# Reading five pair tiles before the last experts, and summing two token tiles at a time on four quarters of TensorE

## The reference

```
h = rmsnorm(x, g_ffn)
# router: top group of 4, then the top 2 of its 8 experts; gates w2 from two softmaxes
act = silu(h @ w_gate[e]) * (h @ w_up[e]) * gate     # 32 experts, 1024 -> 128
x = x + sum over the token's two experts of act @ w_down[e]      # 128 -> 1024
y = x * rsqrt(mean(x * x) + 1e-6) * g_final
```

## Time and profile before

| | |
|---|---|
| median of 3 runs | 610.31 us (609.31 to 610.90) |
| the profiled execution | 608.55 us |
| its span, first to last instruction | 606.5 us |
| busy share of the span | PE 94%, PEld 78%, DVE 73%, ACT 40%, POOL 15% |
| chain that ended last | PE 51%, DVE 17%, DMA 7%, issue 3%, ACT 2% |
| HBM | 96.36 MB read, 21.86 MB written |

### The profile page before, as it was taken

How to read it: one execution, slowest core, us unless ns; L and a number is a source line. 1 busy time by engine, 2 the same in 40 slices (tenths; PEclk the granted TensorE clock), 3 DMA queues, 4 the chain that set the end, 5 groups by cost and what they waited for, 6 DMA issues and landing times.

```text
span 606.5 us, 9765 instructions
## 1 busy us (share of the span) xinstructions
PE 571.4 (94%) x3401; PEld 473.4 (78%) x3401; DVE 439.9 (73%) x749; ACT 242.2 (40%) x389; POOL 88.5 (15%) x136
## 2 busy tenths in 40 slices
PE   8899999999999999899999995899997999999775
PEld 6799999997899889688888874777654768887222
DVE  4937997999999696746666658899731667786285
ACT  6642112222212427322222116576322567775443
POOL 4300000200000000100000000433331334431000
PEclk9999999999999999999999997899998999999889
DMA  8761210131112202455422107699989999962697
GB/s 317 150 123 38 69 36 1 36 93 35 36 36 79 105 36 69 114 203 198 157 80 93 54 36 247 215 332 404 392 329 412 407 352 395 394 241 97 209 421 299
DMA packets 52598, 111.27 MB, mean 183 GB/s; under 512 B 10867, under 2 KB 29176, under 8 KB 51449
## 3 DMA queue, kind: packets, MB, share of 16 engines
q1 hardware_dynamic: 44773, 92.18, 43.2%
q0 software_dynamic: 7168, 17.84, 8.2%
q10 hardware_dynamic: 596, 0.50, 0.3%
HBM read 96.36 MB, written 21.86 MB: 195 GB/s over the span
## 4 chain that ended last, share of the span: by engine, by line
PE 51%; DVE 17%; DMA 7%; issue 3%; ACT 2%; SPq 1%; POOL 0%; POOLq 0%; DVEq 0%; ACTq 0%
PE ps L2259 14%; PE ps L2081 9%; PE ps L2425 6%; PE ps L2364 3%; PE ps L2386 3%; PE ps L2400 3%; PE ps L2401 3%; PE ps L2402 3%; DMA at_opair_p<-scratch_out 3%; DMA at_wlater<-in_expert_w_down 3%; DVE at_mixP L1360 3%; PE ps L2496 2%; PE ps L2323 2%; DVE at_hT L1319 1%; DVE at_lnsq L1546 1%
## 5 line engine op out<-in xcount | busy, mean ns | idle before, releaser
L2081 PE MATMUL ps<-at_hT,at_ring 128*128 128x384 f32 x936 | 165.5, 333 | 0.0
L2081 PEld LDWEIGHTS ps<-at_hT,at_ring 128*128 128x128 f32 x936 | 155.9, 188 | 5.1 <-issue 5.0
L2259 PE MATMUL ps<-at_hT,at_mring 128*128 128x512 f32 (+1 forms) x432 | 102.7, 393 | 2.0 <-DVE at_mring L1514 1.3
L2259 PEld LDWEIGHTS ps<-at_hT,at_mring 128*128 128x128 f32 (+1 forms) x432 | 77.3, 182 | 21.3 <-DVE at_mring L1514 1.7
L1360 DVE SCALAR_TENSOR_TENSOR at_mixP<-at_uc,at_par,at_mixP 128x1024 f32<-128x1024 f32 x60 | 77.1, 1285 | 2.1
L2400 PE MATMUL ps<-at_whi,at_hTm 128*128 128x256 f32 x176 | 51.0, 290 | 0.0
L2402 PE MATMUL ps<-at_whi,at_hTm_lo 128*128 128x256 f32 x176 | 49.1, 279 | 0.0
L2364 PEld LDWEIGHTS ps<-sb_ident,at_xg 128*128 128x128 f32 x232 | 29.3, 192 | 18.2 <-issue 15.2
L1795 DVE TENSOR_TENSOR at_wlater_lo<-at_wlater,at_whi 128x1024 fp32r<-128x1024 f32 x30 | 36.7, 1225 | 6.0 <-ACT at_whi L988 5.1
L2425 PE MATMUL ps<-at_wlater,at_actT 128*128 128x512 f32 (+1 forms) x92 | 38.0, 597 | 0.7 <-ACT at_actT L1003 0.7
L988 ACT ACTIVATE at_whi<-at_wlater 128x1024 fp32r<-128x1024 f32 x30 | 31.6, 1055 | 7.3 <-PE ps L2402 6.5
(11 more groups left out here) (324 smaller groups left out, 919.2 us busy)
## 6 DMA issues: line engine op xcount, KB each, us to landing
at_wlater<-in_expert_w_gate SPq DMA_DIRECT2D x20, 512.0 KB, 11.1
at_wlater<-in_expert_w_up SPq DMA_DIRECT2D x20, 512.0 KB, 12.8
at_wlater<-in_expert_w_down SPq DMA_DIRECT2D x20, 512.0 KB, 15.4
at_raw<-in_w_in SPq DMA_DIRECT2D x16, 512.0 KB, 4.0
at_opair_p<-scratch_out SPq DMA_DIRECT2D x8, 1024.0 KB, 14.7
at_wfirst<-in_expert_w_gate SPq DMA_DIRECT2D x12, 512.0 KB, 9.0
at_wfirst<-in_expert_w_up SPq DMA_DIRECT2D x12, 512.0 KB, 10.0
at_wfirst<-in_expert_w_down SPq DMA_DIRECT2D x12, 512.0 KB, 12.5
```

What stands on the lines that cost most here:

```text
L2081: mm = pe.matmul(ps[:, bank + r, 0:t1 - t0], w[:, wpart, k * P:(k + 1) * P], hT[:, hpart, k, t0:t1], start=(m, wpart, hpart) == (0, 0, 0), ...
L2259: mm = pe.matmul(ps[0:n, b + r, :], mring[:, 1 - i % 2, mpart, k * P:k * P + n], wo[:, wpart, k, r * 512:(r + 1) * 512], start=(c, mpart, ...
```

## The change

1. **Early reads.** SP no longer reads all pairs after `moe_done`. `HELD` = 4: once the scatters of blocks 0 to 24 have landed, it reads the pairs of tiles 0 to 4 (`EARLY`), tile 4 also after block 25's down product. POOL waits for these five reads before it scatters block 25. The outputs of blocks 26 and 27 go to buffers of their own (`kept`) instead of `outb`, and the last four scatters always take 128 rows.
2. **Late rows.** Once everything has landed, POOL gathers into the same tiles those tokens' pairs that had an output in the last four blocks (`late_pairs`, five indirect DMAs of 8 KB rows, by the list `later`; other tokens have an index out of bounds and are skipped). VectorE makes the list in blocks 14 to 16 (`pair_turns`, `pair_latest`, `pair_lists`). SP reads tiles 8, 7, 5, 6 (`WHOLE`) after `moe_done` as before.
3. **A filled scratch.** Since rows are read before they are all written, SP first fills `orow` with rows of the inputs: ten DMAs from HBM to HBM behind the pieces 5 to 13, eight of 1 MB and two of 256 KB.
4. **Quarters.** All eight prompt tiles are summed on TensorE, two at a time: (0, 1), (2, 3), (4, 7), (5, 6). As the diagonal matrix and the identity are zero off the diagonal, only the 64 x 64 blocks on it are used: quarter (q, n) multiplies rows 64q to 64q + 63 of tile n of the couple into PSUM partitions 64n to 64n + 63 of double bank 2c + q. A bank so holds half of one tile and half of the other, and each result tile is written by two DMAs of 64 rows. Only tile 8 stays on VectorE.
5. **Gates** are computed in block 17, and ScalarE makes 16 diagonals right behind the last block's output; a one-element copy on VectorE (`dve_clear`) lets TensorE begin with `own_rows`.

The core of the diff:

```diff
-FINAL = [8, 0, 1, 2, 3, 4, 7, 5, 6]
-PE_TILES = [0, 2, 4, 5, 6]
-DVE_TILES = [8, 1, 3, 7]
+COUPLES = [(0, 1), (2, 3), (4, 7), (5, 6)]
+SUMMED = [i for couple in COUPLES for i in couple]
+EARLY = [0, 1, 2, 3, 4]
+WHOLE = [8, 7, 5, 6]
+HELD = 4
...
+            for p in range(2, NPIECE):
+                load_piece(p)
+                if 5 <= p < 14:
+                    fill_out(p - 5)
...
+            b = NB - HELD - 1
+            for k in range(2):
+                sp.wait_ge(scat[k], 16 * ((b + 2 - k) // 2))
+            for i in EARLY:
+                if i == SUMMED[4]:
+                    sp.wait_ge(s["d_done"], b + 2)
+                load_pairs(i)
...
             sp.wait_ge(s["moe_done"], 1)
-            for i in FINAL:
+            for i in WHOLE:
+                load_pairs(i)
...
+                if b == NB - HELD + 1:
+                    for i in EARLY:
+                        pool.wait_ge(pair_in[i], 16)
                 if b >= 1:
                     scatter(b - 1, columns(b - 1)[1])
...
+            def late_pairs():
+                pool.wait_ge(s["turns_ready"], 1)
+                for i in EARLY:
+                    g.indirect_dma_start(opair(i), None, pairs,
+                                         bass.IndirectOffsetOnAxis(ap=later[:, i:i + 1], axis=0),
+                                         bounds_check=last_token, oob_is_err=False).then_inc(pair_late[i], 16)
...
             with pool.If(total < 1):
                 all_scattered(NB)
+                late_pairs()
...
+            def quarters(couple, h, stationary, moving, **flags):
+                for q in range(2):
+                    p = slice(q * 64, q * 64 + 64)
+                    for n in range(2):
+                        mm = pe.matmul(sum_banks(2 * couple + q)[n * 64:n * 64 + 64, h, :],
+                                       stationary(n)[p, p], moving(n)[p, :], **flags)
+                return mm
...
+            own_rows(0)
             own_rows(1)
+            for c, couple in enumerate(COUPLES):
+                if c >= 2:
+                    pe.wait_ge(s["y_done"], 2 * c - 1)
+                    own_rows(c)
+                for i in couple:
+                    pe.wait_ge(pair_in[i], 16)
+                    if i in EARLY:
+                        pe.wait_ge(pair_late[i], 16)
+                pe.wait_ge(s["dg_ready"], 4 * c + 4)
                 for h in range(2):
                     for k in range(2):
                         q = k * D + h * 512
+                        mm = quarters(c, h, lambda n: dg[:, 2 * c + n, k, :],
+                                      lambda n: opair(couple[n])[:, q:q + 512], start=False, stop=k == 1)
```

More of the change, by code:

```diff
@@ L294, in build_layer @@
         order = at("order", [P, 8, REST], o_state + 2304)
+        both = at("both", [P, TILES, 2, NE], o_state)
+        turn = at("turn", [P, NE], o_state + 2304)
+        latest = at("latest", [P, TILES, 2], o_state + 2304 + 192)
+        done_by = at("done_by", [P, TILES], o_state + 2304 + 288)
+        token = at("token", [P, TILES], o_state + 2304 + 384)
+        later = at("later", [P, TILES], o_state + 2304 + 672, I32)
+        no_over = at("no_over", [P, 1], o_state + 2304 + 736)
         eid = at("eid", [1, REST], o_state + 3072, I32)
@@ L374, in build_layer @@
         pair_in = [sem(f"pair_in{i}") for i in range(TILES)]
+        pair_late = {i: sem(f"pair_late{i}") for i in EARLY}
         def wait_piece(eng, p):
@@ L1285, in _ @@
                 all_scattered(NB)
+                late_pairs()
             over_from(0)
+            with pool.If(total > 0):
+                pool.wait_ge(s["moe_done"], 1)
+                late_pairs()
         @block.vector
```

238 lines of the change are left out of this document (135 added, 103 removed).

## The result

The changed kernel is slower: 623.0 us median of 4 runs (619.11 to 626.11) against 610.19 (609.31 to 610.9); the ratio is 1.0207, 95% interval 1.0146 to 1.0269. The profiled execution took 619.11 us with a span of 617.4; before it was 608.55 and 606.5.

What follows compares the result with a forecast made beforehand. It took the 43 us serial tail as bound by reads, then TensorE; `moe_done` +5.5 and a tail behind it of 37.7 against 39.1 gave span 610.6 (+4.1), so 614.4 us from the median 610.31; range 608 to 620.5.

Steps and rivals of the forecast that it cites:

- Early reads in at 564.9, held scatters: Last blocks: early reads take 15.5 us, then four held scatters go back to back; `moe_done` at 572.9, 5.5 us later.
- A gather beside the reads lands in 7.4 us: After `moe_done`: tile 1's gather, issued about 574.4 beside SP's reads, lands 7.4 us later, so couple 0 starts at 581.8.
- Quarters, four at once: TensorE's tail sums: four quarters run at once, 3.44 us for a couple's 32 rows, 1.72 for its own rows.
- Half clock in couple 0, 2.1 us: TensorE at couple 0: a slow clock after 11 us of idling adds 2.1 us, making the sum 5.5.
- The chain couple, norms, own rows: Tail: couple 2's own rows wait for couple 0's two norms (4.6 us); couple 3 ends at 602.3, last norms at 606.9.
- The last write, 3.55: End of span: two DMAs of 64 rows, 3.1 us plus 0.45 for the second issue, ending at 610.5.
- What costs nothing: Ahead of the tail: filling `orow` costs 0; the gather list on VectorE 0 to 0.5 us, taken as 0.1.
- 0.1 that I had allowed on VectorE: Blocks 14 to 17: making the list for the gathers was taken to cost 0.1 us, from a range of 0 to 0.5.
- within 0.3%: Rival for the tail, chance 0.23: reads land in 14.1 us and the gather in 3.8, giving 609.5 us.
- faster: Rival, chance 0.17: early reads in by 562.6, `moe_done` at 567.4 to 569, low gather, no cold clock; 606.4 us.
- Row halves do not take turns: Denies a rival for TensorE's quarters, chance 0.08: row halves take turns, adding 16.1 us, 630 us.
- the change does what it says: Denies a rival, chance 0.02: blocks overflow, so the gathers would be of every token.

Runs made afterwards that it cites:

- early_two: The changed kernel with two tiles (0, 1) read early instead of five, the other seven read whole after `moe_done`: 616.25 us, ratio 1.0114.
- no_early: The changed kernel without early reads, held scatters and gathers; quarters, diagonals and filled rows stay: 612.95 us, ratio 1.0044.
- warm: gathers_first plus eleven unused whole float32 matmuls on TensorE between the own rows of couples 0 and 1: 616.61 us, ratio 1.0094.
- gathers_first: The changed kernel, but SP, after reading tile 8, waits for the five gathers to land before reading tiles 7, 5, 6: 615.93 us, ratio 1.0099.
- halves: The kernel before, but each prompt tile is written by two DMAs of 64 rows instead of one of 128: 611.39 us, ratio 1.0029.
- control: The changed kernel once more, nothing edited: 622.88 us, ratio 1.0218.
- last_couple: The kernel before with quarters only for tiles 5 and 6, in banks of their own, written in 64-row pieces: 612.28 us, ratio 1.0059.
- patched_last: The changed kernel with two early tiles (0, 1) summed late, tile 1 last, whole-tile sums as before and 128-row writes: 610.26 us, ratio 1.0014.

## Why the prediction was off

1. **Early reads in at 564.9, held scatters.** Right. POOL went on at 565.59. The four scatters came 1.3 us apart, and the last took 4.52 instead of 3.94. `moe_done` came at 574.01 instead of 572.9: +1.1 us. early_two and no_early show that this hold is the only reason for it being late.
2. **A gather beside the reads lands in 7.4 us.** This is the step that failed, by size. Tile 1's was issued at 575.62 instead of 574.4 and took 11.77; couple 0 started at 587.63 instead of 581.8. Of these 5.8 us the landing is 4.4 and the issue 1.2. I had taken the gathers of activations beside weight reads the earlier trace rows. The cause is the reads (6.30 us with only tile 8's beside it). What sets them apart from weight reads stays open between two things that the runs didn't part: their pieces of 8 KB for a partition and the megabytes queued at once. With both made smaller my figure is nearly met (8.34). The Trainium skill (DMA: Bandwidth & Descriptors, SWDGE vs HWDGE vs iDMA) says that an engine takes turns between the two kinds of queue, and I had read that as half of the engines for POOL. The trace shows no even shares, 4.2% of the time against 71.1% in the first 6 us, and not by count either, 37 packets against 167.
3. **Quarters, four at once.** Right: 3.43 a couple at full clock, 1.72 to 1.95 for its own rows.
4. **Half clock in couple 0, 2.1 us.** Right in kind: 0.50 and 0.55 in 585 to 591. Couples 0 and 1 took 8.60 us, against 7.10 in warm, so it cost 1.5 here and 2.33 in gathers_first. The sum at 586.28 in the earlier trace rows lost 5.40 - 3.70 = 1.7, not the 2.1 that I took.
5. **The chain couple, norms, own rows.** Right: from couple 0's start to the last norm's end I had 606.9 - 581.8 = 25.1 us, and measured 612.72 - 587.63 = 25.1. That it agrees to a tenth is luck: couple 0 itself was 0.3 shorter than I had it, the norms and the last two couples together as much longer. This chain is also why halving TensorE's time gains nothing.
6. **The last write, 3.55.** It took 4.7, +1.15. I had counted the second issue and not the lower rate of pieces of 64 rows; halves, with 4.3, shows that rate.
7. **What costs nothing.** Right in this trace: with block 24's scatter at 545.40, filling and list cost nothing. In the mean of many executions it isn't shown. (The pairs read after `moe_done` in the kernel before are 8.9 MB, not the 8.5 that I wrote; no term uses the figure.)

Couple 0's start, 5.8 us late with `moe_done`'s 1.1 in it, and the last write, 1.15, less 0.1 that I had allowed on VectorE, make the 6.8 us by which the span of 617.4 exceeds my 610.6. The other 1.8 of the 8.6 us in the median lie in how the traced executions stand to their medians. The changed kernel's trace is its fastest run, 3.9 us under its median of 623.0. Before's is 1.8 under the 610.31 that I scaled by, with the half clock at tile 4 in it. (The last 0.3 is time around the span, 1.7 us and not 2.05.) The position of block 24's scatter, 2.6 us later in control, is one reason; how the parts share the rest stays open.

Of the rivals, "within 0.3%" and "faster" both needed landings of 3.8 us; not even with the reads held back did tile 1's gather reach that (6.30). Row halves do not take turns, and the change does what it says.

## What to carry to other kernels

When data is read early and the rest patched by a small transfer, price the patch as it runs: beside the very reads that will run with it, and with the sums that wait for it. Here couple 0 started 13.5 us behind `moe_done` with two tiles patched (early_two) and 11.4 behind it with the same tiles read whole (no_early). A unit made twice as fast gains nothing when its work then waits in pairs, for the later of two landings and for two norms in a row. And read a term that rests on one gap of one execution, such as a fallen clock, in a second trace first.

## What the runs showed of the hardware

- Indirect gathers on POOL's queue beside 3.67 MB of SP's reads: 4.2% of the engines in the first 6 us, landing 10.2 to 13.4 us behind their issue; with three of the four reads held back 36.7% and 5.0 to 7.0. Beside reads in pieces of 4 KB instead of 8 KB for a partition, which are also issued more slowly, tile 1's lands in 8.34 us instead of 11.63; beside two reads at a time in 9.21.
- A DMA whose destination is two stretches of 64 rows used two engines' worth: 53 GB/s instead of 418.
- Writes of 64 partitions moved 254 to 332 GB/s with the engines 0.74 to 0.88 busy (halves), one of 128 partitions 418 (before).
- TensorE's clock fell to half behind 2.32 us of idle and 2.65 us (last_couple), but not behind 2.28 us (halves) or 2.29 (patched_last).
- Four 64x64 float32 quarters with 512 columns run at once, at 0.107 us for a row of 512 (3.43/32).
